# Rotary half swaps and key spreading of a grouped-query attention, moved from TensorE products to DMA transfers on GpSimd's queue

## The chip, the cores and the metric

The kernel runs on one core of one Trainium2 chip, in one launch. The metric is the device time in microseconds. A profile is one execution, taken apart from the timed runs. Engines: TensorE (PE; its weight loads are listed as PEld), VectorE (DVE), ScalarE (ACT), GpSimd (POOL) and SyncE (SP), whose only task here is to issue transfers. Each engine works through its own list of instructions in order, and waits on semaphores where another engine's result is needed. DMA transfers are issued by SP, ACT or GpSimd and run beside all of them; each adds 16 to a semaphore when it has landed.

## The reference

Everything is float32, 512 tokens of width 1024. Two layers of a first block (a latent attention, a gated linear attention and a retention branch side by side, then a gated feed-forward with a short convolution) are followed by one second block with three attention branches. The second of these is the grouped-query branch, the one that is changed: 8 query heads and 2 key heads of 64 features.

```python
qb_ = axial_rope(rms_norm(bq.reshape(b, s, B_HEADS, HEAD_DIM), q_norm[layer]), row_pos, col_pos)
kb_ = axial_rope(rms_norm(bk.reshape(b, s, B_KV_HEADS, HEAD_DIM), k_norm[layer]), row_pos, col_pos)
vb_ = bv.reshape(b, s, B_KV_HEADS, HEAD_DIM)
sc = jnp.einsum('bqkgd,bskd->bkgqs', qc, kb_).astype(jnp.float32) * (HEAD_DIM ** -0.5)
p = jax.nn.softmax(sc, axis=-1).astype(vb_.dtype)
return jnp.einsum('bkgqs,bskd->bqkgd', p, vb_)
```

`axial_rope` splits the 64 features of a head into two groups of 32 and rotates each: `[x1*cos - x2*sin, x1*sin + x2*cos]` with halves of 16 features. So a rotation of a tile needs the tile itself and the same tile with the two halves of 16 features swapped.

## The kernel before

**Layout and products.** Activations lie with features on the 128 partitions and tokens along the free axis, as tiles of 128x512. Projections are made with float32 accuracy out of two rounded parts: a weight chunk arrives by DMA in `w_raw` (two slots), ACT rounds it to `w_hi`, DVE subtracts (`split2`, L2356) and leaves `w_lo`; the activations have such parts too (`h2_hi`, `h2_lo`; `gt_hi`, `gt_lo`). Each output tile of PE is a sum of three products (L863 to L865). A chunk of 256 output columns gives two tiles, `2*c` and `2*c + 1`; `tile2` (L1370) makes one. It waits for the chunk's split and for the copy out of the last tile in its PSUM bank. SP loads chunk `c` once chunk `c - 2` has been split (L969).

**Order.** All orders are written out by hand, engine by engine, and meet at semaphores; no planner is involved. The stretch that matters lies between the first attention's last pair and the grouped-query attention's first score product, near the end of the second block.

**The tiles of the branch.** `q_b` holds five tiles: 0 to 3 are the query heads, two to a tile, and 4 the two key heads. `v_feat` holds the values with features on the partitions, `k_b` the two key heads, each spread over both halves of the partitions, so that the two heads of a pair can meet it at partitions 0 and 64. `late` holds constants, among them the two selection matrices for the spread, the 64-wide block matrix for the norms, and the cosines and sines `ax_cos`, `ax_sin`.

**PE** (from L1433): gate tile `2*C2_GA`; five sums of squares (L1438); gate tile `2*C2_GA + 1`; for tiles 0 to 3 of `q_b` a product with the permutation `swap32`, which leaves the swapped halves in PSUM banks 4 to 7 (`turn_b`, L1442); four transposes of `v_feat` (L1452); gate tile `2*C2_GA + 2`; the swap of tile 4 (it must wait until bank 4 has been read, `roped` 25); gate tile `2*C2_GA + 3`; two products of the roped keys with the selection matrices (L1459); the first tile of the branch merge, `merge_tile(C2_MA, 0, 8)`; then it waits for `k_b` (L1462) and starts the attention with its first score products (L626), behind which the second merge tile follows as `lead`. A float32 product of 128x512 counts as two matmul records.

**DVE** (from L2455): five `norm_b` (L2458, semaphore `h_norm`), then `branch_parts` (L2396) with work put between. For each gate tile `k` it makes the gated product `full` (L2405), then `low(k - 1)` (L837), which needs `gt_hi[k - 1]` from ACT, then what `after[k]` says. After 0 come ropes 0 to 3, after 1 the split of chunk `C2_MA` and rope 4, after 2 the two copies of the spread keys out of PSUM (L2480). A rope is three instructions: times cosine (L2011), swapped times sine (L2013), sum (L2015, semaphore `roped`).

**ACT** (from L1860): squares, factors (L808, L810), a table load, the copies of gate tiles 0 and 1 with the gate function (L1557), the high part of the next chunk (L1816), the copy of the turned values into `v_b` (L1869), then `gt_hi[0]` and `gt_hi[1]` (L826), the copy of gate tile 2, `gt_hi[2]`, and so on.

**GpSimd** issues a few loads at the start, and in each layer of the first block 16 transfers that swap halves of 16 partitions for the retention branch (L1092). After these its list is over. SP issues similar transfers elsewhere (`rot_k`, L982; the spread `kr<-kg`, L979; `swapped`, L1030).

Of the kernel before, what the change touches and what calls it, by code (L numbers as in the profile page):

```python
# [17 lines left out]
P = 128  # L18
S = 512
# [3 lines left out]
DEPTH = 2  # L23
# [101 lines left out]
def build(nc, A, out, PER):  # L125
# [4 lines left out]
    def sem(name):  # L130
        if name not in sems:
            sems[name] = ctx.enter_context(nc.semaphore(name))
        return sems[name]

    with ctx:
# [9 lines left out]
        ident, swap32, causal = (cm[:, i * P:(i + 1) * P] for i in range(3))  # L145
# [23 lines left out]
        def at(name, kib, shape, dt=F32):  # L169
            n = int(np.prod(shape[1:])) * (4 if dt in (F32, F32R) else 2)  # L170
            assert (kib + H_KIB) * 1024 + n <= room, (name, kib, n, room)
            return nc.alloc_sbuf_tensor_at(name, shape, dt, offset=ARENA + int((kib + H_KIB) * 1024))
# [77 lines left out]
        out_sb = at("out_sb", 72, [P, RES, D])  # L250
        y_tok = at("y_tok", -16, [P, RES, D])
        tmp2 = at("tmp2", 92, [P, S])
        v_feat = at("v_feat", -4, [P, S])
        prob_b, prob_bt = at("prob_b", 80, [P, 2, S]), at("prob_bt", 84, [P, 2, S])
        inv_a, norm_a = at("inv_a", -8, [P, S]), at("norm_a", -6, [P, S])
# [11 lines left out]
        layer = {}  # L267
# [3 lines left out]
        def upto(eng, name, k=None):  # L271

            k = count[name] if k is None else k
            return layer[eng] * PER.get(name, 0) + CREDIT.get(name, 0) + k

        def tick(name, by=1):
            count[name] += by
            return by
# [643 lines left out]
        UNITS_B = [(k, part) for k in range(2, 16) for part in ((0, 1) if k % 4 < 2 else (None,))]  # L922
        SLOTS_B = sorted([0] + [3 * p + 1 for p in range(PAIRS)] + [3 * p + 2 for p in (3, 7, 11)])
        STAT_B = (4, 5, 6, 7, T_BANK)
        SLOT_B = dict(zip(SLOTS_B, UNITS_B))

        def slots(*pairs_):
# [138 lines left out]
        @block.gpsimd  # L1066
        def _(pool):

            pool.memset(slot_view(w_raw, 0, KD)[:, :, P + ROPE + GATE_RANK:256], 0.0).then_inc(sem("w_split"), 1)
            pool.memset(ones[:], 1.0).then_inc(sem("w_split"), 1)  # L1070
            pool.wait_ge(sem("w_split"), 2)
            pool.wait_ge(sem("init_x"), 16 * NT)
            pool.dma_start(gains_in[G_CONVW:G_CONVB],
                           A["ffn_conv_w"].rearrange("l w (k p) -> (w k) l p", p=P)).then_inc(sem("init_wide"), 16)
            for name, c0, k in GAINS[5:]:
                pool.dma_start(gains_in[c0:c0 + k], A[name].rearrange("l (k p) -> k l p", p=P)).then_inc(sem("init_wide"), 16)
            with nc.allow_non_contiguous_dma("gains go one to a partition"):
                pool.dma_start(wg_all[64:64 + GATE_RANK], A["gla_w_gate"].rearrange("l r n -> r l n")).then_inc(sem("init_g"), 16)
                for c0, k, src in ((0, 8, A["final_norm"]), (8, 8, A["g_pre_2"][0]), (16, 8, A["g_mem_2"][0]),
                                   (32, 24, A["b_merge_2"][0])):  # L1080
                    pool.dma_start(g2[:, c0:c0 + k], src.rearrange("(k p) -> p k", p=P)).then_inc(sem("init_g"), 16)
                for c, name in ((56, "q_norm_2"), (57, "k_norm_2")):
                    for half in range(2):
                        pool.dma_start(g2[64 * half:64 * half + 64, c:c + 1],
                                       A[name][0].rearrange("(p k) -> p k", k=1)).then_inc(sem("init_g"), 16)

            for l in range(DEPTH):
                layer[pool] = l
                pool.wait_ge(sem("tile_copied"), upto(pool, "tile_copied", 2 * C_UQ + 1))
                for j in range(2):  # L1090
                    for b in range(8):
                        pool.dma_start(rot_l[16 * b:16 * b + 16, j], lin[16 * (b ^ 1):16 * (b ^ 1) + 16, 2 + j]).then_inc(  # L1092
                            sem(f"l_rotated{j}"), 16)

        @block.tensor
        def _(pe):
# [273 lines left out]
            def tile2(t, kind="f", K=KD, hi=h2_hi, lo=h2_lo, n=S, ready=None, part=None):  # L1370

                c, half = t // 2, t % 2
                b = bank2[t]
                if part == 1:
                    features(pe, c % 2, half, K, hi, lo, b, first=False,
                             order=range(K // 2, K)).then_inc(sem("tile_done"), tick("tile_done"))
                    return
                if half == 0:
                    split_ready(c)
                if before2[t] is not None:  # L1380
                    pe.wait_ge(sem("tile_copied"), upto(pe, "tile_copied", before2[t] + 1))
                if part == 0:
                    features(pe, c % 2, half, K, hi, lo, b, last=False, order=range(K // 2))
                    return
                if kind == "f":
                    ins = features(pe, c % 2, half, K, hi, lo, b, n=n, ready=ready)
                elif kind == "t":
                    ins = tokens(pe, c % 2, half, K, hi, lo, b, (2 * half, 2 * half + 1), ready=ready)
                else:
                    ins = tokens(pe, c % 2, half, K, hi, lo, b, (half,))  # L1390
                ins.then_inc(sem("tile_done"), tick("tile_done"))
# [47 lines left out]
                          stop=True).then_inc(sem("stat"), tick("stat"))  # L1439
            tile2(2 * C2_GA + 1)  # L1440

            def turn_b(j):  # L1442
                pe.wait_ge(sem("h_norm"), upto(pe, "h_norm", j + 1))
                if j == 4:
                    pe.wait_ge(sem("roped"), upto(pe, "roped", 25))
                pe.matmul(ps[:, 4 + j % 4, :], swap32, q_b[:, j, :], start=True, stop=True).then_inc(sem("rot"), tick("rot"))

            for j in range(4):
                turn_b(j)
            pe.wait_ge(sem("h_norm"), upto(pe, "h_norm", 5))  # L1450
            for t in range(NT):
                ins = pe.transpose(ps[:, T_BANK, t * P:t * P + P], v_feat[:, t * P:t * P + P], ident)  # L1452
            ins.then_inc(sem("v_turned"), 1)
            tile2(2 * C2_GA + 2)
            turn_b(4)
            tile2(2 * C2_GA + 3)
            pe.wait_ge(sem("roped"), upto(pe, "roped", 29))
            for j in range(2):
                ins = pe.matmul(ps[:, 6 + j, :], late[:, j * P:j * P + P], q_b[:, 4, :], start=True, stop=True)  # L1459
            ins.then_inc(sem("k_spread"), tick("k_spread"))  # L1460
            merge_tile(C2_MA, 0, 8)
            pe.wait_ge(sem("k_b"), upto(pe, "k_b", 2))  # L1462

            def values_kept():
                pe.wait_ge(sem("v_kept"), 1)
# [488 lines left out]
        def _(dve):  # L1954
# [54 lines left out]
            def rope(z, rot, cos, sin, dst, t):  # L2009

                dve.tensor_tensor(dst, z, cos, ALU.mult).then_inc(sem("rope_cos"), tick("rope_cos"))  # L2011
                dve.wait_ge(sem("rope_cos"), upto(dve, "rope_cos"))
                dve.tensor_tensor(t, rot, sin, ALU.mult).then_inc(sem("rope_sin"), tick("rope_sin"))  # L2013
                dve.wait_ge(sem("rope_sin"), upto(dve, "rope_sin"))
                dve.tensor_tensor(dst, dst, t, ALU.add).then_inc(sem("roped"), tick("roped"))  # L2015
                dve.wait_ge(sem("roped"), upto(dve, "roped"))
# [339 lines left out]
            def split2(c):  # L2356

                slot, n = c % 2, second[c][0] * 128
                dve.wait_ge(sem("w_split"), upto(dve, "w_split", c))
                for q in range(2):  # L2360
                    dve.wait_ge(sem("w_high"), upto(dve, "w_high", 2 * c - 1 + q))
                    ins = dve.tensor_tensor(w_lo[:, slot, q * n:q * n + n], w_raw[:, slot, q * n:q * n + n],  # L2362
                                            w_hi[:, slot, q * n:q * n + n].bitcast(F32), ALU.subtract)
                ins.then_inc(sem("w_split"), 1)
# [95 lines left out]
                dve.wait_ge(sem("h_norm"), upto(dve, "h_norm"))  # L2460

            def rope_b(j):
                dve.wait_ge(sem("rot"), upto(dve, "rot", j + 1))
                rope(q_b[:, j], ps[:, 4 + j % 4, :], ax_cos, ax_sin, q_b[:, j], tmp2[:])

            for j in range(5):
                norm_b(j)

            def ropes():
                for j in range(4):  # L2470
                    rope_b(j)

            def last_rope():
                split2(C2_MA)
                rope_b(4)

            def keys_spread():
                dve.wait_ge(sem("k_spread"), upto(dve, "k_spread", 1))
                for j in range(2):
                    dve.tensor_copy(k_b[:, j], ps[:, 6 + j, :]).then_inc(sem("k_b"), tick("k_b"))  # L2480
                    dve.wait_ge(sem("k_b"), upto(dve, "k_b"))

            branch_parts(0, C2_GA, 8, after={0: ropes, 1: last_rope, 2: keys_spread})
            split2(C2_MA + 1)
            pair_dve(dve, b_pairs(), B_BANKS, inv_b, norm_bt,
                     fill=slots((0, partial(split2, C2_MA + 2)), *[(i, partial(merge, 0, C2_MA, k)) for i, (k, part) in SLOT_B.items() if k % 4 > 1],
# [127 lines left out]
```

## Time and profile before

| | |
|---|---|
| runs of the kernel | 2002.37, 2002.53, 2003.14 us; median 2002.53 |
| the profiled execution, its own time | 2004.78 us |
| its span, first to last instruction | 2002.6 us |
| mean granted clock of TensorE | 0.995 of full speed |
| instructions | 29029 |
| GpSimd's queue | 1520 packets, 1.17 MB |

Times in the rows are microseconds from the start of the span, unless marked ns. Busy time is instructions at work; issuing a DMA does not count as busy on the engines' page rows, though a table of stretches shows GpSimd's issues. A number in brackets behind a timeline row is how long the engine had been idle and who ended it. PEclk is the clock that TensorE was granted, 1.00 being full speed. A timeline merges equal instructions and gives their count.

### The profile page before, as it was taken

Reading aid. Unit: us, or ns where it says so; the run is one execution under the profiler, and the core shown is the slowest. Engines: PE = TensorE matmul, PEld = TensorE weight load, DVE = VectorE, ACT = ScalarE, POOL = GpSimd, SP = SyncE. Lnnn points to the kernel's source line nnn. Section 1 sums busy time; section 2 is a strip of 40 time slices with the busy share of each in tenths; the row PEclk is TensorE's granted clock in tenths of the full one; section 3 lists DMA queues with packets and bytes.
Section 4 is the critical chain, followed back from the end, with each engine's and each line's share of the span. In section 5 each row is a group of like instructions: output and inputs, shape, how many; then the busy total and the mean of one; then the engine's idle time right before and its main releaser. Section 6 shows DMA issues by size and latency. Waiting matters only on the chain.

```text
span 2002.6 us, 29029 instructions
## 1 busy us (share of the span) xinstructions
PE 1966.5 (98%) x10962; PEld 1613.9 (81%) x10962; DVE 1150.6 (57%) x1382; ACT 826.2 (41%) x1211; POOL 25.9 (1%) x52
## 2 busy tenths in 40 slices
PE   7999999999999999999999999999999999999998
PEld 5897788888887897788888888987777766798888
DVE  6866765655445866766555445846664633443435
ACT  5445443333223345443333222334445555554444
POOL 2001000000000001000000000000000000000000
PEclk8999999999999999999999999999999999999999
DMA  6213133332224223133332223523332212232222
GB/s 192 75 47 105 43 105 105 84 105 85 94 95 120 69 55 106 43 105 96 93 104 85 95 95 80 183 73 99 89 110 68 63 53 64 84 115 76 92 87 85
DMA packets 239916, 181.26 MB, mean 91 GB/s; under 512 B 12842, under 2 KB 232232, under 8 KB 239422
## 3 DMA queue, kind: packets, MB, share of 16 engines
q1 hardware_dynamic: 237856, 177.37, 29.6%
q0 software_dynamic: 1520, 1.17, 0.3%
q10 hardware_dynamic: 430, 1.23, 0.3%
q8 instruction: 72, 1.18, 0.2%
q14 instruction: 38, 0.31, 0.1%
HBM read 168.21 MB, written 2.10 MB: 85 GB/s over the span
## 4 chain that ended last, share of the span: by engine, by line
PE 88%; DVE 6%; issue 2%; ACT 2%; DMA 1%; SPq 0%; DVEq 0%; ACTq 0%
PE ps L863 24%; PE ps L865 23%; PE ps L864 23%; PE ps L626 2%; PE ps L650 2%; PE ps L639 2%; DVE amat L2087 2%; PE ps L1285 1%; PE ps L1286 1%; PE ps L1287 1%; PE ps L506 1%; PE ps L475 1%; DMA w_raw<-in_w_in_dram 1%; PE ps L1169 1%; PE ps L495 1%
## 5 line engine op out<-in xcount | busy, mean ns | idle before, releaser
L863 PE MATMUL ps<-h_hi,w_hi 128*128 128x512 f32 x1376 | 553.8, 402 | 2.3 <-ACT qk L1557 2.0
L865 PE MATMUL ps<-h_hi,w_lo 128*128 128x512 f32 x1376 | 541.0, 393 | 0.0
L864 PE MATMUL ps<-h_lo,w_hi 128*128 128x512 f32 x1376 | 537.1, 390 | 0.0
L1973 DVE TENSOR_TENSOR w_lo<-w_raw,w_hi 128x2048 fp32r<-128x2048 f32 (+3 forms) x110 | 227.2, 2065 | 225.5 <-ACT w_hi L1564 218.0
L863 PEld LDWEIGHTS ps<-h_hi,w_hi 128*128 128x128 f32 x1376 | 259.4, 189 | 61.0 <-issue 7.4
L865 PEld LDWEIGHTS ps<-h_hi,w_lo 128*128 128x128 f32 x1376 | 259.2, 188 | 59.6
L864 PEld LDWEIGHTS ps<-h_lo,w_hi 128*128 128x128 f32 x1376 | 259.5, 189 | 56.0 <-issue 1.9
L1564 ACT ACTIVATE w_hi<-w_raw 128x2048 fp32r<-128x2048 f32 (+3 forms) x108 | 186.8, 1729 | 232.4 <-PE ps L865 211.9
L2362 DVE TENSOR_TENSOR w_lo<-w_raw,w_hi 128x1024 fp32r<-128x1024 f32 (+1 forms) x118 | 126.5, 1113 | 167.4 <-ACT w_hi L1816 166.7
L863 PE MATMUL ps<-w_hi,h_hi 128*128 128x256 f32 x544 | 152.4, 280 | 0.3 <-DVE h_lo L837 0.2
L864 PE MATMUL ps<-w_lo,h_hi 128*128 128x256 f32 x544 | 150.7, 277 | 0.0
L865 PE MATMUL ps<-w_hi,h_lo 128*128 128x256 f32 x544 | 150.7, 277 | 0.0
L863 PE MATMUL ps<-hid_hi,w_hi 128*128 128x512 f32 x352 | 138.7, 394 | 0.0
L865 PE MATMUL ps<-hid_hi,w_lo 128*128 128x512 f32 x352 | 138.0, 392 | 0.0
L864 PE MATMUL ps<-hid_lo,w_hi 128*128 128x512 f32 x352 | 136.6, 388 | 0.0
L1816 ACT ACTIVATE w_hi<-w_raw 128x1024 fp32r<-128x1024 f32 (+1 forms) x118 | 108.3, 965 | 4.1 <-issue 2.2
L863 PEld LDWEIGHTS ps<-w_hi,h_hi 128*128 128x128 f32 x544 | 102.3, 188 | 1.9 <-DVE h_lo L837 0.7
L1765 ACT ACTIVATE rms_a<-a_pad,g 128x512 f32<-128x512 f32 x44 | 35.9, 817 | 162.5 <-DVE a_pad L2298 162.5
L864 PEld LDWEIGHTS ps<-w_lo,h_hi 128*128 128x128 f32 x544 | 102.3, 188 | 0.1
L865 PEld LDWEIGHTS ps<-w_hi,h_lo 128*128 128x128 f32 x544 | 102.2, 188 | 0.0
L2303 DVE SCALAR_TENSOR_TENSOR rms_a<-a_pad,g,rms_a 128x512 f32<-128x512 f32 x88 | 66.2, 752 | 58.3 <-ACT rms_a L1765 51.7
L865 PEld LDWEIGHTS ps<-hid_hi,w_lo 128*128 128x128 f32 x352 | 66.1, 188 | 15.5
(390 smaller groups left out, 2767.6 us busy)
## 6 DMA issues: line engine op xcount, KB each, us to landing
w_raw<-in_ffn_w_up_dram SPq DMA_DIRECT2D x88, 512.0 KB, 4.6
w_raw<-in_w_in_dram SPq DMA_DIRECT2D x41, 1024.0 KB, 5.3
w_raw<-in_w_in_dram SPq DMA_DIRECT2D x32, 512.0 KB, 5.2
w_raw<-in_ffn_w_down_dram SPq DMA_DIRECT2D x32, 512.0 KB, 4.0
w_raw<-in_w_out_dram SPq DMA_DIRECT2D x12, 1024.0 KB, 5.6
w_raw<-in_ffn_w_down_dram SPq DMA_DIRECT2D x16, 384.0 KB, 3.4
swapped<-qk SPq DMA_DIRECT2D x96, 64.0 KB, 2.0
w_raw<-in_w_mem_kv_dram SPq DMA_DIRECT2D x4, 1024.0 KB, 5.8
```

Of the source, the lines that this page charges most:

```text
L626: ins = pe.matmul(ps[:, b, c:c + n], lhs, rhs, start=True, stop=True)
L639: ins = pe.transpose(ps[:, T_BANK + c // 512, c % 512:c % 512 + P], probs[:, e, c:c + P], ident)
L650: ins = pe.matmul(ps[64 * e:64 * e + 64, O_BANK, r * P:r * P + P], pairs[p].pv[e][k], probs_t[:, e, k * P:k * P + P], start=(k == 0), stop ...
L863: pe.matmul(dst, lh, rh, start=first and j == 0, stop=False)
L864: pe.matmul(dst, lh, rl, start=False, stop=False)
L865: ins = pe.matmul(dst, ll, rh, start=False, stop=last and j == len(order) - 1)
L1564: act.activation(w_hi[:, slot, 0:n], w_raw[:, slot, 0:n], ACT.Copy).then_inc(sem("w_high"), 1)
L1816: act.activation(w_hi[:, slot, q * n:q * n + n], w_raw[:, slot, q * n:q * n + n], ACT.Copy).then_inc(sem("w_high"), 1)
L1973: dve.tensor_tensor(w_lo[:, slot, 0:n], w_raw[:, slot, 0:n], w_hi[:, slot, 0:n].bitcast(F32), ALU.subtract).then_inc(sem("w_split"), 1)
L2087: dve.copy_predicated(amat[:].rearrange("p h t n -> p (h t) n"), levels[:, lv:lv + 1, :].to_broadcast([P, 4 * NT, P]), ps[:, MAIN:MAIN + 4 ...
L2303: dve.scalar_tensor_tensor(conv[:], a_pad[:, s, w:w + S], g[:, bass.ds(G_CONVW + w * KF + f, 1)], conv[:], ALU.mult, ALU.add).then_inc(sem ...
L2362: ins = dve.tensor_tensor(w_lo[:, slot, q * n:q * n + n], w_raw[:, slot, q * n:q * n + n], w_hi[:, slot, q * n:q * n + n].bitcast(F32), AL ...
```

## The change

The five products with `swap32` go. Instead GpSimd, once a tile has been normed, issues eight transfers of 16 partitions for it, which write the swapped tile into a new buffer `rot_b` in SBUF, over space that the first attention has left. The two products with the selection matrices and the two copies behind them go too: GpSimd waits for the last rope and issues four transfers of 64 partitions that write `k_b`. PE waits for those four instead of for DVE's copies. Two orders change with it. On PE gate tile `2*C2_GA + 2` comes ahead of the transposes of `v_feat`. On DVE ropes 0 and 1 follow gated product 0, the split of chunk `C2_MA` and rope 2 follow product 1, and ropes 3 and 4 follow product 2.

```diff
+        rot_b = at("rot_b", -16, [P, 5, S])
...
+        B_ROTATED = ("b_rotated0", "b_rotated1", "b_rotated2", "l_rotated0", "l_rotated1")
...
+            layer[pool] = 2
+            for j in range(5):
+                pool.wait_ge(sem("h_norm"), upto(pool, "h_norm", j + 1))
+                for b in range(8):
+                    pool.dma_start(rot_b[16 * b:16 * b + 16, j], q_b[16 * (b ^ 1):16 * (b ^ 1) + 16, j]).then_inc(
+                        sem(B_ROTATED[j]), 16)
+            pool.wait_ge(sem("roped"), upto(pool, "roped", 29))
+            for j in range(2):
+                for half in range(2):
+                    pool.dma_start(k_b[64 * half:64 * half + 64, j], q_b[64 * j:64 * j + 64, 4]).then_inc(sem("k_spread"), 16)
...
-            def turn_b(j):
-                pe.wait_ge(sem("h_norm"), upto(pe, "h_norm", j + 1))
-                if j == 4:
-                    pe.wait_ge(sem("roped"), upto(pe, "roped", 25))
-                pe.matmul(ps[:, 4 + j % 4, :], swap32, q_b[:, j, :], start=True, stop=True).then_inc(sem("rot"), tick("rot"))
-
-            for j in range(4):
-                turn_b(j)
+            tile2(2 * C2_GA + 2)
             pe.wait_ge(sem("h_norm"), upto(pe, "h_norm", 5))
             for t in range(NT):
                 ins = pe.transpose(ps[:, T_BANK, t * P:t * P + P], v_feat[:, t * P:t * P + P], ident)
             ins.then_inc(sem("v_turned"), 1)
-            tile2(2 * C2_GA + 2)
-            turn_b(4)
             tile2(2 * C2_GA + 3)
-            pe.wait_ge(sem("roped"), upto(pe, "roped", 29))
-            for j in range(2):
-                ins = pe.matmul(ps[:, 6 + j, :], late[:, j * P:j * P + P], q_b[:, 4, :], start=True, stop=True)
-            ins.then_inc(sem("k_spread"), tick("k_spread"))
             merge_tile(C2_MA, 0, 8)
-            pe.wait_ge(sem("k_b"), upto(pe, "k_b", 2))
+            pe.wait_ge(sem("roped"), upto(pe, "roped", 28))
+            pe.wait_ge(sem("k_spread"), 16 * 4)
...
             def rope_b(j):
-                dve.wait_ge(sem("rot"), upto(dve, "rot", j + 1))
-                rope(q_b[:, j], ps[:, 4 + j % 4, :], ax_cos, ax_sin, q_b[:, j], tmp2[:])
+                dve.wait_ge(sem(B_ROTATED[j]), 128 + (0 if j < 3 else DEPTH * PER["l_rotated0"]))
+                rope(q_b[:, j], rot_b[:, j], ax_cos, ax_sin, q_b[:, j], tmp2[:])
...
-            def ropes():
-                for j in range(4):
+            def ropes(first, last):
+                if first == 2:
+                    split2(C2_MA)
+                for j in range(first, last):
                     rope_b(j)
 
-            def last_rope():
-                split2(C2_MA)
-                rope_b(4)
-
-            def keys_spread():
-                dve.wait_ge(sem("k_spread"), upto(dve, "k_spread", 1))
-                for j in range(2):
-                    dve.tensor_copy(k_b[:, j], ps[:, 6 + j, :]).then_inc(sem("k_b"), tick("k_b"))
-                    dve.wait_ge(sem("k_b"), upto(dve, "k_b"))
-
-            branch_parts(0, C2_GA, 8, after={0: ropes, 1: last_rope, 2: keys_spread})
+            branch_parts(0, C2_GA, 8, after={0: partial(ropes, 0, 2), 1: partial(ropes, 2, 3), 2: partial(ropes, 3, 5)})
```

## Rows read from the trace of the kernel before

**Rows 1.** The page, part 1: busy us (share of the span) and instructions of TensorE.
```profile
PE 1966.5 (98%) x10962; PEld 1613.9 (81%) x10962; DVE 1150.6 (57%) x1382; ACT 826.2 (41%) x1211; POOL 25.9 (1%) x52
```

**Rows 2.** Table of stretches: us, busy of each engine, PEclk, DMA share, GB/s.
```profile
1541.00:1560.00 19.00, 19.00 (x74) 12.87 (x71) 9.35 (x12) 16.14 (x23) 0.00 (x0) 1.00 0.37 122
1560.00:1581.00 21.00, 21.00 (x88) 15.15 (x86) 18.23 (x26) 7.45 (x11) 0.00 (x0) 1.00 0.16 51
```

**Rows 3.** The chain that ended last, 1556 to 1582: start us, us, what.
```profile
1557.03 3.43 PE ps L1446 x8
...
1560.46 0.44 PE ps L1452 x4
...
1566.40 0.86 PE ps L1446 x2
...
1572.77 1.85 PE ps L1459 x4
...
1580.12 1.06 PE ps L626 x4
```

**Rows 4.** Timeline of ACT: start us, us, engine, line, instruction [idle before].
```profile
1556.39 1.33 ACT L1557 ACTIVATE sgate_a<-ps 128x512 f32<-128x512 f32 x2
...
1560.93 0.60 ACT L1869 ACTIVATE v_b<-ps 128x512 f32<-128x512 f32 x1 [1.18 <-PE ps L1452]
...
1561.57 0.63 ACT L826 ACTIVATE gt_hi<-full 128x512 fp32r<-128x512 f32 x1
```

**Rows 5.** Timeline of DVE, the same stretch.
```profile
1549.67 0.75 DVE L2458 SCALAR_TENSOR_TENSOR q_b<-q_b,g,rms_a 128x512 f32<-128x512 f32 x1 [5.11 <-ACT rms_a L810]
...
1557.09 0.69 DVE L2405 TENSOR_TENSOR full<-o_br,sgate_a 128x512 f32<-128x512 f32 x1 [1.16 <-ACT sgate_a L1557]
...
1557.99 0.69 DVE L2011 TENSOR_TENSOR q_b<-q_b,late 128x512 f32<-128x512 f32 x1 [0.21 <-PE ps L1446]
...
1560.17 0.69 DVE L2011 TENSOR_TENSOR q_b<-q_b,late 128x512 f32<-128x512 f32 x1
...
1568.16 2.36 DVE L2362 TENSOR_TENSOR w_lo<-w_raw,w_hi 128x1024 fp32r<-128x1024 f32 x2
```

**Rows 6.** Table of stretches: GpSimd's 16 issues in layer 1; DVE around the ropes.
```profile
148.93:156.61 7.68, 7.68 (x35) 6.28 (x35) 3.87 (x6) 3.60 (x6) 7.68 (x16) 1.00 0.61 163
1557.10:1575.40 18.30, 18.30 (x71) 12.57 (x70) 16.79 (x23) 7.00 (x11) 0.00 (x0) 1.00 0.18 57
```

**Rows 7.** Timeline of ACT before the first of those issues.
```profile
148.04 0.60 ACT L1557 ACTIVATE qr<-ps 128x512 f32<-128x512 f32 x1 [0.26 <-PE ps L865]
```

**Rows 8.** GpSimd's transfers of L1092: duration ns min/median/max, and time to landing.
```profile
L1092 POOL DMA_DIRECT2D rot_l<-lin x32: 487/487/507, 148.9 to 758.4; - x32
...
DMA to landing us min/median/max: 2.0/2.4/2.6
```

**Rows 9.** GpSimd's issues of L1084: duration ns min/median/max.
```profile
L1084 POOL DMA_DIRECT2D g<-in_q_norm_dram x2: 536/543/550, 17.5 to 18.1; - x2
```

**Rows 10.** DMA issues by line, of the whole kernel: count, KB each, median us to landing.
```profile
kr<-kg SPq DMA_DIRECT2D x4, 128.0 KB, 2.3
...
rot_k<-kg SPq DMA_DIRECT2D x8, 64.0 KB, 2.0
```

**Rows 11.** SyncE's swapped transfers of the first attention (L1030): time to landing.
```profile
DMA to landing us min/median/max: 1.9/2.0/3.3
```

**Rows 12.** Table of stretches: TensorE's spells at the lower clock.
```profile
20.12:23.92 3.80, 3.80 (x9) 2.79 (x10) 3.49 (x6) 3.80 (x9) 0.00 (x0) 0.50 0.82 73
1621.36:1624.78 3.42, 3.42 (x10) 2.65 (x9) 1.25 (x2) 1.92 (x5) 0.00 (x0) 0.50 0.58 184
1716.75:1720.17 3.42, 3.42 (x11) 2.65 (x11) 0.00 (x0) 3.17 (x9) 0.00 (x0) 0.53 0.70 226
```

**Rows 13.** Timeline of TensorE: the first work before the two late spells.
```profile
1620.40 0.63 PE L639 MATMUL ps<-cm,prob_b 128*128 128x128 f32 x4 [1.97 <-ACT prob_bt L697]
...
1715.30 1.69 PE L1476 MATMUL ps<-cm,mem_in 128*128 128x128 f32 x8 [2.18 <-ACT mem_t L1889]
```

## The prediction

> **What bounds the kernel now.** I read the page first: TensorE (PE) is busy for 98% of the span [rows 1], so the question for every stretch is whether PE works or waits there. Then the table of stretches around the change: from 1541 to 1581 us PE has no idle time at all, at full clock, while VectorE (DVE) is busy for 18.2 of the last 21 us, GpSimd does nothing and the DMA engines are nearly empty [rows 2]. So work taken off PE here is worth its whole length, unless something else is late at the next meeting point. That point is the first score product of the grouped-query attention (L626), which needs the spread keys `k_b`; it starts at 1580.12 us [rows 3]. The chain of the last work, in order of time, names what PE would lose [rows 3]; the timelines of ScalarE (ACT) and DVE in the same stretch say how fast the others can follow [rows 4, 5].
>
> The changed time is set by two sums: when PE is ready for L626, and when `k_b` is.
>
> **Removed from PE.** Four swap products are 3.43 us of the chain, the fifth 0.86, the two spreads 1.85 [rows 3]: 6.14 us. The four transposes of `v_feat` (0.44 us) only move behind tile `2*C2_GA+2`. PE is then ready at 1580.12 - 6.14 = 1573.98 us. The two copies of the keys on DVE (L2480) go as well; they stand behind PE's product and in front of nothing that I find late, so I take them at nothing.
>
> **When are the keys ready?** Step by step, starting with the transfers of the swapped halves.
> - GpSimd sees the first norm done at 1549.67 + 0.75 = 1550.42 us [rows 5], and starts about 0.29 us after that: in layer 1 its queue started at 148.93 [rows 6] and the copy that it waited for ended at 148.04 + 0.60 = 148.64 [rows 7]. So 1550.7.
> - It issues 5 x 8 = 40 transfers of 16 partitions, like the 16 of L1092 that took 7.68 us in a row, 0.48 each [rows 6, 8]. The later norms are no brake: DVE finishes all five before 1557.09 [rows 5], and the queue is at its 14th issue there. The last one starts at 1550.7 + 39 x 0.48 = 1569.4 and lands 2.4 us later [rows 8]: 1571.8. Tile 1 (16th issue) lands at 1560.3, tile 2 at 1564.1, tile 3 at 1568.0.
> - DVE: gated product 0 from 1557.09 [rows 5], rope 0 from 1557.8 (its halves landed at 1556.5). A rope is three instructions, 1560.17 - 1557.99 = 2.18 us [rows 5]. Rope 1 waits for its transfer until 1560.3 and ends at 1562.5; gated product 1 ends at 1563.2.
> - Now DVE must wait for ACT: `low(0)` needs `gt_hi[0]`, and ACT first copies the turned values (L1869). PE turns them after tile `2*C2_GA+2` now: the tile can start when the first gate copy is over, 1556.39 + half of 1.33 = 1557.1 [rows 4], takes 1566.40 - 1560.90 = 5.5 us (between the end of the transposes, 1560.46 + 0.44, and the fifth swap [rows 3]), then 0.44: 1563.04. ACT: 0.60 for the values, 0.63 for `gt_hi[0]` [rows 4]: 1564.4. This wait is new, about 1.2 us of DVE, and the chain to the keys runs through it.
> - DVE from 1564.4: `low(0)` 0.73, split of chunk `C2_MA` 2.3 [rows 5], rope 2 2.18, gated product 2 and `low(1)` 1.46, ropes 3 and 4 4.36. Sum 11.0: the keys are roped at 1575.4. Rope 4 starts at 1573.2 and its halves are there at 1571.8, a margin of 1.4 us.
> - GpSimd wakes (0.29) and issues 4 transfers of 64 partitions. No row has this form from GpSimd. Near it: issues of 64 partitions with a tiny payload take 0.54 us [rows 9], those of 16 partitions 0.487 [rows 8], and I take 0.52; landing of 32 KB from its queue takes 2.0 to 2.6 us [rows 8]; on SyncE's queue 128 KB land in 2.3 and 64 KB in 2.0 [rows 10], so the size adds 0.3 or more. I take 2.8, nearest to 2.4 plus that. The fourth lands at 1575.4 + 0.29 + 3 x 0.52 + 2.8 = 1580.05. Bounds: 1575.4 + 3 x 0.487 + 2.0 = 1578.9, and with the slowest landing of SyncE's swapped transfers, 3.3 [rows 11], 1580.6.
>
> So PE, ready at 1573.98, waits: tile `2*C2_MA` is done, and nothing else stands in front of L626. It goes on at 1580.1, within 0.1 us of where it stood. The 6.14 us are turned into a stall of about 6.1 us: **the expected gain is nothing** (bounds -1.2 and +0.5 us). What the new wait holds up on PE is everything behind it, beginning with the second tile of the merge; ACT and DVE need PE's scores next, and they shift with it. The weight loads on SyncE wait for DVE's splits; the split of chunk `C2_MA` comes some 3 us earlier, so the loads are no later. The weight load that it sets off runs beside the last swapped halves, at 1567 to 1573; the 1.4 us margin covers that up to the 3.3 us landing of [rows 11].
>
> **The clock.** A stall costs more than its length. PE's granted clock is 0.50 to 0.53 (1.2 GHz) in three stretches [rows 12], and the two late ones stand right behind idle PE, of 1.97 us and 2.18 us [rows 13]; PE works there for 3.42 us at half speed and so loses 1.7 us each. At the start, after idle time with the input loads, it works 3.80 us at half speed, 1.9 us lost [rows 12]. The new stall is three times as long as the two, so I count one such spell behind it: +1.8 us. Bounds: nothing, and two spells in a row, 3.6 us. The two late spells themselves may move, vanish or find company once everything is a little shifted: 1.7 us each, either way, taken at zero.
>
> **Sum.** 6.14 less on PE, 6.1 stall, 1.8 clock: +1.8 us. The profiled execution took 2004.78 us by the clock outside its span of 2002.6, the three runs a median of 2002.53 us; I apply the difference to the median: **2004.3 us**, which nobody could tell from no change: 0.2%, about what a measurement of this kernel can tell, is 4.0 us, so 1998.5 to 2006.5.
>
> **A rule that speaks against the change.** While GpSimd issued its 16 transfers, DVE was busy for 3.87 of the 7.68 us, with six instructions (0.65 us each on average) of kinds that read two operands from SBUF, and no issue took over 507 ns [rows 6, 8]. The ropes keep DVE busy for 16.79 of 18.30 us [rows 6]. The Trainium skill (GPSIMD Engine Reference, Key points) says that GpSimd shares its SBUF interfaces with VectorE and contends with instructions that have two SBUF inputs. By that rule the third rival below, at its upper end, would be the likeliest, and the sum 2014; by the row, issues run at 0.48 us and the sum stands.
>
> **Rivals.**
> 1. The wait is there but the clock hardly costs, or a later spell vanishes: 2001 to 2003 us, at the centre 2002.5. For it: the late spells are only two among many short waits of PE in that stage. Against it: the gap is long, and the next work of PE is continuous. 17%.
> 2. The clock stays low for two spells: 2004.3 + 1.8 = 2006.1. 9%.
> 3. Slower than before: GpSimd's queue becomes the bound. Place: the 40 issues in front of rope 4. Rope 4 can start at 1573.2, so the turning point is a pace of (1573.2 - 2.4 - 1550.7) / 39 = 0.515 us an issue, only 7% over the 0.48 seen; beyond it each 0.01 us costs 0.39. At 0.54 [rows 9] it costs +1.0: 2005.3. If each issue had to find its place between two DVE instructions (0.727 us apart, a third of 2.18), the last would land at 1550.7 + 39 x 0.727 + 2.4 = 1581.5 and rope 4 start 8.3 us late: with a second clock spell 2014. Against it: [rows 6, 8]. 14%.
> 4. The change does not do what it says, PE going on early as the transfers were ready in time. For that the keys would have to be in `k_b` by 1574; they are only roped at 1575.4, and the fastest landing is 2.0. To be faster by 4 us needs the keys at 1574.3 even with no loss of clock. 2%.
>
> The forecast itself has 58%. **Chances:** faster by over 0.2% 2%; within 0.2% the forecast, rival 1, most of rival 2 and a little of rival 3, 78%; slower by more 20% (rival 3 mostly, the upper ends of rival 2 and of the forecast). The range takes the low end of the keys with no loss of clock, 2002.5 - 1.2 = 2001.3, a little lower for a spell that vanishes; and above 2004.3 + 0.5 + 1.9 + 1.7 = 2008.4 (late keys, a second spell, one new one). 2001.0 to 2008.5.
>
> **What would show it.** In the changed profile: L626 first starts near 1580.1, with some 6 us of idle PE before it put down to a DMA into `k_b`; granted clock 0.50 for the next 3 to 4 us of work; L1446 and L1459 gone; DVE waiting for ACT before `low(0)`; 44 more issues on GpSimd of about 0.48 us; no long wait of DVE for the last `rot_b`. Waits of several us of rope 3 or 4 on a DMA mean rival 3. A first score before 1576, or a stall under 3 us, would prove me wrong.

## The result, and the profile after

The changed kernel takes 2006.3 us (median of 20 runs, 2004.32 to 2013.34), the kernel before 2003.26 us (20 runs, 2001.46 to 2006.12): ratio 1.0015, 95% interval 1.0008 to 1.0022, that is +3.0 us (1.6 to 4.4): small, but clear of no change. In the set of runs of e1, e2, e7 and e8 below one run of the kernel before (2450 us) and one of e1 (2181 us) fell into a slower state of the chip; the ratios leave them out, the medians do not. The profiled execution took 2007.90 us, its span is 2006.1 us, against 2004.78 and 2002.6 before.

The two traces run side by side until the branch begins: the first gated product starts at 1556.90 us, at 1557.09 before [rows 5]. The chain that ended last, 1545 to 1592 us, names everything behind it (start us, us, what; L627, L864 to L866 are lines 626, 863 to 865 of before):

```profile
1549.48 0.76 DVE q_b L2458
1550.24 0.28 issue
1550.52 18.55 POOL rot_b L1100 x39
1569.07 5.12 DMA rot_b<-q_b
1574.28 0.70 DVE q_b L2011
...
1575.73 0.70 DVE q_b L2015
1576.43 0.28 issue
1576.72 1.55 POOL k_b L1105 x3
1578.26 2.69 DMA k_b<-q_b
...
1581.09 2.08 PE ps L627 x4
1583.16 0.72 PE ps L864
1583.88 0.43 PE ps L865
...
1586.44 0.24 PE ps L865
```

Where [rows 3] had PE alone, the chain now runs through GpSimd's queue, a transfer, DVE, the queue again, a transfer, and only then PE. In PE's timelines the first scores, before and after, are

```profile
1580.05 1.13 PE L626 MATMUL ps<-k_b,q_b 64*128 64x512 f32 x4
```

```profile
1581.09 2.08 PE L627 MATMUL ps<-k_b,q_b 64*128 64x512 f32 x4 [6.94 <-DMA k_b<-q_b]
```

They start at 1581.09 instead of 1580.05 (1580.12 in the chain of [rows 3]), and PE's products behind them take 0.43 us each instead of 0.23, until 1586.4. The timeline of DVE shows the two waits on the way:

```profile
1564.54 0.69 DVE L838 TENSOR_TENSOR gt_lo<-full,gt_hi 128x512 fp32r<-128x512 f32 x1 [1.86 <-ACT gt_hi L827]
...
1574.28 0.69 DVE L2011 TENSOR_TENSOR q_b<-q_b,late 128x512 f32<-128x512 f32 x1 [0.97 <-DMA rot_b<-q_b]
```

The table of stretches (us, busy PE, PEld, DVE, ACT, POOL with counts, PEclk, DMA share, GB/s), against [rows 2]:

```profile
1541.00:1560.00 19.00, 18.90 (x75) 13.65 (x76) 9.69 (x13) 15.95 (x23) 9.48 (x20) 1.00 0.54 153
1560.00:1573.90 13.90, 13.90 (x64) 11.29 (x62) 11.08 (x15) 5.78 (x9) 9.55 (x21) 1.00 0.52 127
1573.90:1581.09 7.19, 0.25 (x3) 0.04 (x1) 5.45 (x8) 1.67 (x3) 2.08 (x4) 0.65 0.30 74
1581.09:1586.20 5.11, 5.11 (x11) 2.97 (x12) 1.38 (x2) 1.56 (x4) 0.00 (x0) 0.50 0.33 106
```

PE is full until 1573.9, as if the products were simply gone, idles for 6.94 us from 1574.15 on, and then works for 5.1 us at half clock, which costs it 2.55 us. The clock had already fallen inside the stall (0.65 on average there). So the 3.5 us between the two spans are 1.0 at the first scores (1.2 if both are counted from the first gated product) and 2.5 behind them: from the first scores to the end it is 2006.1 - 1581.09 = 425.0 us, and 2002.6 - 1580.05 = 422.5 before.

GpSimd's transfers, by tile: durations of the issues, then the time to landing of those into `rot_b`.

```profile
L1100 POOL DMA_DIRECT2D rot_b<-q_b x40: 484/484/487, 1550.5 to 1569.1; - x40
...
DMA to landing us min/median/max: 1.7/1.8/5.4
```

The pace is what [rows 8] had, but the landing has a tail: 1.8 us mostly, 5.4 at worst. The tail lies at the end: the first 36, issued up to 1567.2 us, land in 1.7 to 2.0 us, the last four, issued from 1567.6 on, in 3.7 to 5.4. At 1567.65 stands SyncE's load of a 1 MB weight chunk, in the timeline of its queue:

```profile
1567.65 0.37 SPq L974 DMA_DIRECT2D w_raw<-in_w_in_dram  x1
```

### The profile page after: what moved, and what is told of

The parts are those of the page before. It is cut to its first block, busy times and chain, and to the rows that moved or that the text cites. A ratio compares the mean times of both kernels' runs of the same rounds, so it can differ in the third digit from the quotient of the medians.

```text
span 2006.1 us, 29042 instructions
## 1 busy us (share of the span) xinstructions
PE 1962.2 (98%) x10948; PEld 1612.0 (80%) x10948; DVE 1148.8 (57%) x1380; ACT 825.6 (41%) x1211; POOL 47.0 (2%) x96
## 4 chain that ended last, share of the span: by engine, by line
PE 87%; DVE 6%; issue 2%; ACT 2%; POOL 1%; DMA 1%; ACTq 0%; DVEq 0%; SPq 0%
PE ps L864 23%; PE ps L866 23%; PE ps L865 23%; PE ps L627 2%; PE ps L651 2%; PE ps L640 2%; DVE amat L2087 2%; PE ps L1297 1%; PE ps L1299 1%; PE ps L1298 1%; PE ps L507 1%; POOL rot_b L1100 1%; PE ps L476 1%; PE ps L1181 1%; PE ps L901 1%
## 5 line engine op out<-in xcount | busy, mean ns | idle before, releaser
L864 PE MATMUL ps<-h_hi,w_hi 128*128 128x512 f32 x1376 | 553.0, 402 | 2.4 <-ACT qk L1557 2.0
L866 PE MATMUL ps<-h_hi,w_lo 128*128 128x512 f32 x1376 | 540.9, 393 | 0.0
L864 PEld LDWEIGHTS ps<-h_hi,w_hi 128*128 128x128 f32 x1376 | 259.5, 189 | 61.7 <-issue 8.9
L866 PEld LDWEIGHTS ps<-h_hi,w_lo 128*128 128x128 f32 x1376 | 259.0, 188 | 59.4
L864 PE MATMUL ps<-w_hi,h_hi 128*128 128x256 f32 x544 | 152.4, 280 | 0.3 <-DVE h_lo L838 0.2
L866 PE MATMUL ps<-w_hi,h_lo 128*128 128x256 f32 x544 | 150.7, 277 | 0.0
L864 PE MATMUL ps<-hid_hi,w_hi 128*128 128x512 f32 x352 | 138.7, 394 | 0.0
L866 PE MATMUL ps<-hid_hi,w_lo 128*128 128x512 f32 x352 | 138.0, 392 | 0.0
L864 PEld LDWEIGHTS ps<-w_hi,h_hi 128*128 128x128 f32 x544 | 102.4, 188 | 1.9 <-DVE h_lo L838 0.7
L866 PEld LDWEIGHTS ps<-w_hi,h_lo 128*128 128x128 f32 x544 | 102.1, 188 | 0.0
L866 PEld LDWEIGHTS ps<-hid_hi,w_lo 128*128 128x128 f32 x352 | 66.1, 188 | 15.5
```

Of the source, the lines that this page charges most:

```text
L864: pe.matmul(dst, lh, rh, start=first and j == 0, stop=False)
L866: ins = pe.matmul(dst, ll, rh, start=False, stop=last and j == len(order) - 1)
```

## Experiments

My theory: the time is set by the later of two things, PE being ready (1574) and the keys being in place; the keys are late because the key tile is the last in every order; and the stall costs a spell of low clock on top. Rivals: GpSimd's pace; the landing of transfers by itself; a transfer on this path always costing PE something; the clock costing nothing. Ratios are against the kernel before in the same set of runs. Since the executions reach the branch up to 3 us apart, I compare the traces by the distance from DVE's first gated product to the first score product; each trace is a single execution. The edit of e1 is shown against the kernel before, all others against the changed kernel.

| kernel | first gated product | first scores | distance | scores to end | time, ratio (95% interval) |
|---|---|---|---|---|---|
| before | 1557.09 | 1580.05 | 22.96 | 422.5 | |
| changed | 1556.90 | 1581.09 | 24.19 | 425.0 | 1.0015 (1.0008 to 1.0022) |
| e5, PE busy in the stall | 1556.18 | 1580.23 | 24.05 | 421.2 | 1.0006 (0.9996 to 1.0016) |
| e4, weight load later | 1556.74 | 1584.09 | 27.35 | 426.2 | 1.0031 (1.0021 to 1.0041) |
| e6, 24 issues for 40 | 1557.17 | 1580.55 | 23.38 | 425.3 | 1.0019 (1.0009 to 1.0029) |
| e3, transposes first | 1555.51 | 1578.96 | 23.45 | 426.4 | 1.0008 (0.9998 to 1.0017) |
| e1, spread alone | 1558.71 | 1579.82 | 21.11 | 420.8 | 0.9993 (0.9984 to 1.0002) |
| e2, swaps alone | 1556.26 | 1579.20 | 22.94 | 424.1 | 1.0003 (0.9994 to 1.0013) |
| e7, keys first | 1557.99 | 1575.25 | 17.26 | 424.1 | 0.9979 (0.9969 to 0.9988) |
| e8, keys first, late ropes | 1557.50 | 1574.65 | 17.15 | 420.9 | 0.9971 (0.9958 to 0.9983) |

### e5: PE kept busy while it waits

```diff
             pe.wait_ge(sem("roped"), upto(pe, "roped", 28))
+            wh = slot_view(w_hi, C2_MA % 2, KD)
+            for k in range(28):
+                pe.matmul(ps[:, 6, :], wh[:, k % KD, P:2 * P], h2_hi[:, k % KD, :], start=True, stop=True)
             pe.wait_ge(sem("k_spread"), 16 * 4)
```

> The changed kernel with PE kept busy while it waits for the keys: 28 products of already loaded operands into a PSUM bank that nobody reads (28 x 0.229 = 6.4 us of the 6.9 us wait). Nothing else changes and the output is the same. Theory (clock): the wait itself still ends at 1581.1 us of the span, but TensorE's granted clock stays at 1.00 behind it, so the 10 us at 0.50 are gone and the time falls by about 2.5 us against the changed kernel, to 2003.8. Rival (the loss is only the wait, the clock costs nothing): the time stays at 2006.3. Rival (the extra products delay the scores): above 2006.3.

Measured: 2004.75 us, before 2003.81 beside it. The first scores come at the same distance as in the changed kernel (24.05 against 24.19), and the table of stretches has

```profile
1573.20:1580.23 7.03, 6.64 (x30) 5.10 (x29) 5.44 (x8) 1.66 (x3) 2.08 (x4) 1.00 0.32 78
1580.23:1586.20 5.97, 5.97 (x25) 4.36 (x26) 1.38 (x2) 1.56 (x4) 0.00 (x0) 1.00 0.28 88
```

The same wait with PE at work, and full clock behind it. From the scores to the end it is 421.2 us, 3.8 less than in the changed kernel. Two spells make that up, and PE's next long wait, the one of [rows 13], parts them (changed kernel, then e5):

```profile
1623.88 1.09 PE L640 MATMUL ps<-cm,prob_b 128*128 128x128 f32 x4 [1.97 <-ACT prob_bt L698]
```

```profile
1620.58 0.63 PE L640 MATMUL ps<-cm,prob_b 128*128 128x128 f32 x4 [1.97 <-ACT prob_bt L698]
```

From the first scores to there it is 42.79 us in the changed kernel and 40.35 in e5, as in the kernel before: the new spell alone, 2.4 us. The rest is most of the spell near 1621 [rows 12], which did not come in this execution. So the traces show the clock's part of the loss, 2.4 to 2.5 us, against the rival that it costs nothing. The timed runs agree without proving it: 2003.8 was expected, and the ratios to before (1.0006 and 1.0015) are 1.8 us apart, but their intervals overlap. That useless products make the kernel faster is no advice, but the cheapest proof of what the stall costs beside its length.

### e4: the weight load held back

```diff
+                if c == C2_MA + 2:
+                    sp.wait_ge(sem("roped"), upto(sp, "roped", 29))
                 load(c, c % 2, parts, K)
```

> The changed kernel, with SyncE's load of weight chunk C2_MA + 2 (1 MB) held back until the last rope is done. Theory (the last swapped halves landed 5.1 us after their issue because that load ran beside them): the transfers into rot_b all land in about 2 us, DVE does not wait before the last rope, which starts at 1573.4 instead of 1574.3, and the first score product comes at 1580.1 instead of 1581.1; about -1 us, 2005.3. Rival (GpSimd's queue backs up by itself after 40 issues): the last landing stays near 5 us, the rope and the scores stay where they are. Rival (the load is missed later): a new wait of ACT for w_raw and a later time.

Measured: 2011.19 us, the slowest of all, where 2005.3 was expected. Half of the expectation holds, and shows the cause of the tail; by tile, time to landing into `rot_b`:

```profile
DMA to landing us min/median/max: 1.7/1.8/2.1
```

With no load beside them all 40 land in about 2 us, the last like the first, so the queue does not back up by itself; the last rope starts without a wait. The other half was a miss: the load now ran beside the four transfers that spread the keys. Time to landing into `k_b`, and PE's first scores:

```profile
DMA to landing us min/median/max: 6.3/6.5/6.7
```

```profile
1584.09 2.08 PE L627 MATMUL ps<-k_b,q_b 64*128 64x512 f32 x4 [10.02 <-DMA k_b<-q_b]
```

6.5 us instead of 2.7. The load that was moved off one small transfer fell onto the next, which nothing covers. I had asked whether the load would be missed later, not what it would run beside.

### e6: 24 issues instead of 40

```diff
-            for j in range(5):
-                pool.wait_ge(sem("h_norm"), upto(pool, "h_norm", j + 1))
+            for j, t in enumerate((slice(0, 1), slice(1, 3), slice(3, 5))):
+                pool.wait_ge(sem("h_norm"), upto(pool, "h_norm", t.stop))
                 for b in range(8):
-                    pool.dma_start(rot_b[16 * b:16 * b + 16, j], q_b[16 * (b ^ 1):16 * (b ^ 1) + 16, j]).then_inc(
+                    pool.dma_start(rot_b[16 * b:16 * b + 16, t], q_b[16 * (b ^ 1):16 * (b ^ 1) + 16, t]).then_inc(
...
-                dve.wait_ge(sem(B_ROTATED[j]), 128 + (0 if j < 3 else DEPTH * PER["l_rotated0"]))
+                dve.wait_ge(sem(B_ROTATED[(j + 1) // 2]), 128)
```

> The changed kernel with 24 issues on GpSimd instead of 40: tile 0 alone, then tiles 1 and 2 in one set of eight transfers of 64 KB, then tiles 3 and 4. Theory (the keys are late by DVE's own order, with one us of it from the queue): the last issue starts near 1562, lands before the weight load begins, rope 4 starts at 1573.4, first score 1580.1, about -1 us: 2005.3. Rival (GpSimd's pace is the main thing): the first score moves by several us, and the time by as much. Rival (bytes, not issues, set the landing): the landing grows to 3 us or more and rope 1 waits.

Measured: the first scores come 0.8 us nearer (23.38 against 24.19), and rope 4 follows rope 3 without a wait. The queue is done 7.6 us sooner (24 issues in 11.42 us) and the keys gain 0.8: GpSimd's queue, its pace and the late landing at its end together, was one microsecond of the matter, not more. The time, 2007.98 us where 2005.3 was expected, does not show the gain (before 2003.81 beside it; the interval of the ratio is 4 us wide, and a spell of the clock more or less outweighs 0.8 us).

### e3: the transposes back in front

```diff
-            tile2(2 * C2_GA + 2)
             pe.wait_ge(sem("h_norm"), upto(pe, "h_norm", 5))
...
             ins.then_inc(sem("v_turned"), 1)
+            tile2(2 * C2_GA + 2)
```

> The changed kernel with the transposes of v_feat put back ahead of gate tile 2*C2_GA + 2, as they were before. Theory (two chains end at the last rope, DVE's own and the transfers'): DVE's wait of 1.9 us for gt_hi[0] goes, but the split and so the weight load come earlier too, and the last swapped halves still land at 1573 to 1574, so the wait before the last rope grows and the first score moves by 0 to 1 us: 2005.3 to 2006.3. Rival (DVE's wait for ACT was what made the keys late): the first score comes 1.9 us earlier, 2004.4.

Measured: 2006.56 us; the scores come 0.7 us nearer. DVE's wait of 1.86 us for ACT is gone, and

```profile
1572.11 0.69 DVE L2011 TENSOR_TENSOR q_b<-q_b,late 128x512 f32<-128x512 f32 x1 [2.01 <-DMA rot_b<-q_b]
```

the wait for the last swapped halves has doubled from 0.97 to 2.01. Two chains end at the last rope within a microsecond of each other, DVE's own order and the transfers with the load beside them; mending one leaves the other. Both at once were not tried.

### e1: the spread alone

```diff
+            layer[pool] = 2
+            pool.wait_ge(sem("roped"), upto(pool, "roped", 29))
+            for j in range(2):
+                for half in range(2):
+                    pool.dma_start(k_b[64 * half:64 * half + 64, j], q_b[64 * j:64 * j + 64, 4]).then_inc(sem("k_spread"), 16)
...
             tile2(2 * C2_GA + 3)
+            merge_tile(C2_MA, 0, 8)
             pe.wait_ge(sem("roped"), upto(pe, "roped", 29))
-            for j in range(2):
-                ins = pe.matmul(ps[:, 6 + j, :], late[:, j * P:j * P + P], q_b[:, 4, :], start=True, stop=True)
-            ins.then_inc(sem("k_spread"), tick("k_spread"))
-            merge_tile(C2_MA, 0, 8)
-            pe.wait_ge(sem("k_b"), upto(pe, "k_b", 2))
+            pe.wait_ge(sem("k_spread"), 16 * 4)
```

(DVE's two copies go as well.)

> The kernel before with the second part of the change alone: the swaps stay products on TensorE, in the old orders, and only the spreading of the keys goes to four transfers on GpSimd's queue; the two products and DVE's two copies go. Theory: the last rope ends at 1572.6 as before, the transfers (0.28 + 1.6 + 2.7) bring the keys at 1577.2, and TensorE is ready for the first scores at 1580.12 - 1.85 = 1578.3, so nothing waits and no clock spell follows: 1.85 us faster than before (ratio 0.9991). Rival (a transfer on this path costs TensorE a wait in any case): a wait in front of L626 and no gain.

Measured: 2002.99 us, before 2003.68 beside it. By the trace exactly the two products are gained: 21.11 against 22.96, 1.85 us, with PE full over the whole stretch:

```profile
1558.71:1579.82 21.11, 21.11 (x87) 15.44 (x85) 17.80 (x25) 9.37 (x13) 2.09 (x4) 1.00 0.25 75
```

The times agree (ratio 0.9993) but don't separate it from no change. Here, too, the four transfers ran beside a weight load and took longer, in the DMA issues by line:

```profile
k_b<-q_b POOLq DMA_DIRECT2D x4, 128.0 KB, 3.5
```

but the rope ended early enough to cover it, if only just: they were issued from 1574.49 on, so the last landed at about 1579.5 (1574.49 + 3 x 0.52 + 3.5), and the scores began at 1579.82. A transfer on this path costs PE nothing by itself.

### e2: the swaps alone

```diff
-            for j in range(2):
-                for half in range(2):
-                    pool.dma_start(k_b[64 * half:64 * half + 64, j], q_b[64 * j:64 * j + 64, 4]).then_inc(sem("k_spread"), 16)
...
-            pe.wait_ge(sem("roped"), upto(pe, "roped", 28))
-            pe.wait_ge(sem("k_spread"), 16 * 4)
+            pe.wait_ge(sem("roped"), upto(pe, "roped", 29))
+            for j in range(2):
+                pe.matmul(ps[:, 6 + j, :], late[:, j * P:j * P + P], q_b[:, 4, :], start=True,
+                          stop=True).then_inc(sem("k_spread"), tick("k_spread"))
+            pe.wait_ge(sem("k_b"), upto(pe, "k_b", 2))
```

(DVE's two copies follow its last `low(3)`.)

> The changed kernel with the first part alone: the swaps by transfers, but the keys spread by the two products and the two copies of before, placed behind the first merge tile. Theory (DVE's order and the transfers make the last rope late, at 1576.4, against 1572.6 before): TensorE waits from 1574.0 to 1576.5, the spread takes 1.85 us and the copies follow DVE's last gated product, so the first scores come near 1580.1, and a clock spell follows: 1 to 3 us slower than before (ratio 1.0010). Rival (the four spreading transfers make the keys late, 4.5 us from the last rope): TensorE hardly waits, and the time is 2 to 4 us below before.

Measured: 2004.89 us, before 2003.68; 1 to 3 us slower was expected, and the ratio, 1.0003, has 1 within its interval. In the timeline of PE:

```profile
1575.57 1.98 PE L1459 MATMUL ps<-q_b,late 128*128 128x512 f32 x4 [2.09 <-DVE q_b L2014]
...
1579.20 1.13 PE L627 MATMUL ps<-k_b,q_b 64*128 64x512 f32 x4 [1.65 <-DVE k_b L2477]
```

The 4.29 us of swap products are gone, and the scores stand at the old distance (22.94 against 22.96): PE waits for the rope and again for the copies, and from about 1580.9 to 1584.4 it works at half clock. With the spread by transfers, in the changed kernel, it is 24.19. So the part of the change that turns a gain into a wait is the one with the swaps and the order of the ropes, not the four spreading transfers; behind a late rope these only add a microsecond.

### e7: the key tile first

```diff
+        B_ORDER = (4, 0, 1, 2, 3)
...
+                n = B_ORDER[j]
                 for b in range(8):
-                    pool.dma_start(rot_b[16 * b:16 * b + 16, j], q_b[16 * (b ^ 1):16 * (b ^ 1) + 16, j]).then_inc(
+                    pool.dma_start(rot_b[16 * b:16 * b + 16, n], q_b[16 * (b ^ 1):16 * (b ^ 1) + 16, n]).then_inc(
                         sem(B_ROTATED[j]), 16)
+                if j == 2:
+                    pool.wait_ge(sem("roped"), upto(pool, "roped", 25))
...
-            pe.wait_ge(sem("roped"), upto(pe, "roped", 28))
+            pe.wait_ge(sem("roped"), upto(pe, "roped", 26))
...
+                    roped={4: 27, 8: 28, 12: 29},
```

(Behind the wait for `roped` 25 follow the four transfers into `k_b`. Squares, norms and ropes go through the tiles in `B_ORDER` as well.)

> The changed kernel with the key tile first through squares, norms, swapped transfers and ropes, and its spread issued behind the third tile's transfers; queries 1 to 3 are waited for only by the pair that needs them. Theory: the keys land near 1567 and the first scores start at 1574, as soon as TensorE is ready; but DVE, still at its ropes, reaches the first maximum only near 1579.5, so the first turned probabilities come at 1582 and TensorE, done with the next tile at 1580.6, waits 1 to 2 us: 4 to 5 us faster than before (ratio 0.998). Rival (TensorE's stage is bound by something else): the first scores at 1574 but the second pair no earlier than before.

Measured: 2000.63 us, before 2003.68: ratio 0.9979, 4.2 us faster. The scores follow PE's last tile at once (17.26, 5.7 us nearer than before). Then, as expected, DVE comes late to the first maximum, and the transposes behind the next tile wait 1.4 us:

```profile
1583.49 0.65 PE L640 MATMUL ps<-cm,prob_b 128*128 128x128 f32 x4 [1.40 <-ACT prob_b L691]
```

Part of that lateness is the old fault in a new place: the last rope, now that of query tile 3, stood 1.81 us for its swapped halves, which again landed beside the load (5.2 us at worst). I had not expected this.

### e8: and three ropes moved into the attention's loop

```diff
-        rot_b = at("rot_b", -16, [P, 5, S])
+        rot_b = [at(f"rot_b{j}", kib, [P, S]) for j, kib in enumerate((-14, -8, -6, -2, -16))]
...
-            branch_parts(0, C2_GA, 8, after={0: partial(ropes, 0, 2), 1: partial(ropes, 2, 3), 2: partial(ropes, 3, 5)})
+            branch_parts(0, C2_GA, 8, after={0: partial(ropes, 0, 2), 1: partial(split2, C2_MA)})
...
-                     fill=slots((0, partial(split2, C2_MA + 2)), *[(i, partial(merge, 0, C2_MA, k)) for i, (k, part) in SLOT_B.items() if k % 4 > 1],
+                     fill=slots((0, partial(split2, C2_MA + 2)), (2, partial(rope_b, 2)), (5, partial(rope_b, 3)), (8, partial(rope_b, 4)), *[(i, partial(merge, 0, C2_MA, k)) for i, (k, part) in SLOT_B.items() if k % 4 > 1],
```

(All of e7's edits are in it too.)

> As the last one, with the ropes of query tiles 1 to 3 moved into the attention's loop on DVE (their swapped halves lie in other places, since merged takes the old ones). Theory: DVE reaches the first maximum 6.5 us sooner, no new wait is left on TensorE, and the whole 6.14 us of products are gained: ratio 0.997, about 1997.7 where before is 2003.8. Rival (the transfers' queue, beside weight loads, makes a rope in the loop late): a wait of PE or DVE for rot_b in the loop and less than 4 us gained.

Measured: 1997.85 us, before 2003.68: ratio 0.9971 (0.9958 to 0.9983), 5.8 us faster than before, and by the two ratios about 9 faster than the changed kernel. Against e7 the intervals overlap, so what the moved ropes add is shown by the trace alone. PE has no gap of note from the first gated product up to 1600, and the clock holds:

```profile
1557.50:1574.65 17.15, 17.11 (x76) 13.84 (x77) 12.50 (x17) 9.37 (x13) 14.75 (x31) 1.00 0.59 146
1574.65:1600.00 25.35, 25.35 (x141) 17.94 (x141) 15.96 (x23) 14.62 (x29) 0.00 (x0) 1.00 0.27 85
```

17.15 against 22.96 is 5.8 of the 6.14 us of products. The same transfers on the same queue, and the same slow landing at their end (5.2 us at worst), which now meets a rope that nobody waits for.

## Why the prediction was right

- **What PE loses**: 6.14 us off its path, ready at 1573.98. It was full until 1573.9 and idle from 1574.15; e8 gains 5.8 of them.
- **GpSimd's queue**: start 1550.7, pace 0.48, last issue 1569.4; measured 1550.5, 0.476 (18.55 us for 39), 1569.1. The rule that spoke against the change did not come true. All 40 issues took 484 to 487 ns while DVE was at its norms and ropes, busy for 11.08 of 13.90 us from 1560 on. The Trainium skill (GPSIMD Engine Reference, Key points) has contention with instructions of two SBUF inputs; here it cannot be seen in these issues.
- **DVE's order**: the wait for `gt_hi[0]` (1.2 forecast, 1.86 measured: rope 1 did not wait for its halves, since they landed in 1.8 us and not 2.4), low(0) at 1564.4 (1564.5), rope 4 possible at 1573.2 (1573.3).
- **Landing of the last swapped halves, mis-sized**: "the 1.4 us margin covers that up to the 3.3 us landing" was the step that failed. It took 5.1 us, and rope 4 was 0.97 us late. I had named the load beside it and priced it with the worst landing that another queue's transfers had shown, in a stretch that need not have had such a load.
- **The spread**: issues 0.52 apart (0.52), landing 2.8 (2.7), wake-up 0.29 (0.28).
- **The keys**: 1580.1 forecast, 1581.1 in the trace, 1.2 later when both are counted from the first gated product; the rope's delay is all but 0.2 of it.
- **The clock, mis-sized**: 1.8 forecast, 2.55 measured. A stall three times as long brought a longer spell: half clock through 5.1 us of work instead of 3.4 to 3.8. The bound of 3.6 covered it; e5 shows the part. Why the longer stall brings a longer spell stays open.

Sum forecast +1.8 (0 + 1.8), measured +3.0 by the medians and +3.5 by the spans (1.0 + 2.5). Both errors have the same sign and each is about a microsecond. The measured 2006.3 is nearly the number of the second rival (2006.1, 9%), yet not by its mechanism: there was one spell, longer than forecast, and the keys were late as well. The median lies in the range; relative to the 2003.26 us of before in the larger set of runs it stands nearer to my case than the 2006.3 against 2004.3 suggest, as 0.7 us of the difference are the baseline's. That nobody could tell it from no change did not hold: the interval of the ratio leaves out 1. The third rival (queue bound by its pace) is out; e6 shows it. One sum in the fourth was wrong: to be faster by 4 us the keys must come at 1574.3 with the 1.8 us of the clock, and at 1576.1 without. It changes nothing, since roped at 1575.4 they could not have landed before 1577.4.

## What to carry to other kernels

Work taken off a full engine is worth only what the next meeting point leaves of it: add up when that engine will be ready and when what it waits for will be there, and change the order first, so that what it waits for (here the key tile) goes first through every queue. A small transfer that is waited for should not run beside a bulk load unless something covers the longer landing, as in e1; and before a load is moved one asks what it will run beside then. Price a stall of TensorE of several microseconds with its clock spell, 2.5 us here on top of 7.

## What the runs showed that I had not expected

- Landing beside a 1 MB load: 32 KB from GpSimd's queue 1.8 us alone, 5.1 to 5.4 for the last three beside it in the changed kernel; 128 KB 2.7 alone, 3.5 in e1, 6.5 in e4, where that load was issued at 1575.44, just before them, and the next, of 512 KB, at 1578.95. The Trainium skill (DMA: Bandwidth & Descriptors, Queues, rings and completion order) says that each DMA engine takes turns between its queues packet by packet. No run here shows how many turns a transfer waits; what it costs in all is 0.8 us in e1, 3.3 in the changed kernel and 3.8 in e4.
- Without a load beside them these transfers land faster than the same form did in the first block: 1.8 against 2.4 us [rows 8]; why was not tried.
- The spell near 1621 us [rows 12] is absent in e1, e5 and e8 and there in before, the changed kernel, e2, e3, e4, e6 and e7; such a spell is worth about 1.7 us in "scores to end". The wait of PE in front of it is 1.97 us in e1, e5 and e8 as well, so its length does not decide; whether the spell comes may hang on how the work falls in time, which was not tried by itself. The spell is a part of the scatter between runs, and why a gain of 1 us, as in e3 and e6, can be read in a trace but not in medians of ten runs.
- Of the time from the scores to the end, e3 and e4 take 1.4 and 1.2 us more than the changed kernel. It arises behind the second wait of [rows 13], near 1715, far from the edits; its cause stays open.
